# Rounded three-product projections in the first layer, with token halves kept in the gates' buffer

## The chip, the cores and the metric

The kernel runs on one core of a Trainium2 chip. The metric is the device time of one execution in microseconds. An execution's time is its span, from the first instruction to the last, and a little around it. On TensorE (PE in the profile) the matmuls run, VectorE is DVE, ScalarE is ACT, GpSimd is POOL, and SyncE is SP; SP and POOL also issue transfers (DMA).

## The reference, cut to what matters

A transformer of three layers, 512 tokens wide 1024, float32. The first layer begins so (the rest of the model is not touched):

```python
h = _rmsnorm(x, attn_norm[i])                 # 512 x 1024
proj = jnp.matmul(h, w_in[i])                 # 1024 x (512+128+512+64+8+1536+1024+1024)
q_a, c_kv, q_idx, k_idx, w_idx, qkv_b, gate_a, gate_b = _split_cols(proj)
c_kv = _rmsnorm(c_kv, kv_norm[i])
...
score = einsum("bqhs,bqh->bqs", relu(q_idx . k_idx), w_idx)
_, idx = lax.top_k(score, n_sel)              # 128 of the keys for each query
...                                           # attention on the chosen keys, a second branch with q_b, k_b, v_b
```

## The kernel before

Everything is kept transposed: a token tile is `HA[:, k]`, 128 features by 512 tokens, `k` from 0 to 7 (`DT`). The weights lie in HBM in chunks of 128 partitions by 1024 numbers (512 KB). A chunk is eight 128 x 128 blocks, the whole depth of one 128-wide output tile. SP streams the chunks into a ring of eight slots (`RING`, L333): the load of chunk n waits until the first matmul of chunk n-7 has been counted in `chunk_begun`. Chunks 0 to 5 are the compressed keys, the index keys and four index queries; 6 to 9 the queries of branch a; 10 to 21 queries, keys and values of branch b; 22 holds the two small matrices `uk` and `uv`.

What TensorE does, in its program's order (`body` of the tensor block):
- `norm_sum` (L474), then six calls of `linear` (L463): a bank of PSUM gets eight float32 matmuls of 128x128 weights by 512 tokens. The first tile waits for each normed tile (`fresh`).
- 32 small matmuls with `WIDX` (L493), a norm (L498), the bias vector (L502), the index scores (L514, 24 matmul groups, each waiting for ScalarE and VectorE), and eight flips of the bias rows (L521), which read `BIAS_FLIPPED`.
- 12 calls of `linear` (queries of both branches, keys of branch b), then four value chunks (L530). For values the tokens are the stationary side and the weights move: 32 matmuls a chunk that move 128 columns each.
- The `ukuv` chunk (L542 to L551), then the first attention (L1038 to L1067).

A float32 matmul shows as two records in the trace. ScalarE moves each finished bank out (`evac`, L1236); `bank()` lets TensorE start on a bank when its last content has been moved out (four banks in turn).

VectorE norms the tokens (`rms`, L1662), scales the small product, folds the index scores (L1722, L1724), and then takes the 128 highest per query in a long chain of its own (L1734 `max`, L1735 `match_replace`, three score tiles). It needs the first layer's projections again only at L1874. GpSimd loads constants, sends the bias vector to HBM and back (L2212, L2215), masks the scores (L2200) and then waits for `staged` (L2222), set by VectorE at L1874.

Later parts of the kernel (the second and third layer's feed-forward, L743 and L756, and the retention layer, L946 and L991) already compute in three rounded products. There a weight chunk is split into a high half, rounded to the type fp32r by ScalarE (`high`, L1609), and a low half, the difference, made by GpSimd in the chunk's own ring slot (`low`, L2324). TensorE then adds high x high, low x high and high x low (`take_parts` waits for `w_lo`). The halves of the tokens are made once, by ScalarE (high) and VectorE (low, L1704). The high halves of weights have two or four slots; `high` waits, by `chunk_begun` or by the place where it stands, until a slot's last user is done.

Areas: all big tiles share one buffer of 34688 numbers per partition (`area`, and `part` for the fp32r view of the same memory). `GATES` is at 11264 to 19455, written only in the first attention (L1894); `QB` and `KB` at 5120 to 9215, `KA` and `VA` at 19456 to 23551, `WIDX` at 19456.

```python
            def high(n, i=None, place=IN_MLP, slots=None):          # L1603, ScalarE
                turn, back = n // SLOTS + 1, (slots or len(place[0])) - 2
                act.wait_ge(chunk_full[n % SLOTS], (turn if i is None else i + turn) * 16)
                if slots is None or slots > 0:
                    act.wait_ge(S["chunk_begun"], n - back if i is None else i * SLOTS + n - back)
                fn(high_slot(n, place), RING[:, n % SLOTS], ACT.Copy).then_inc(S["w_hi"], 1)

            def low(n, place):                                      # L2321, GpSimd
                pool.wait_ge(S["w_hi"], w.next("w_hi"))
                g.tensor_tensor(RING_LOW[:, n % SLOTS], RING[:, n % SLOTS], high_slot(n, place), ALU.subtract).then_inc(S["w_lo"], 1)
```

## Time and profile before

| what | us |
|---|---|
| median of 3 runs (2671.18 to 2673.55) | 2673.55 |
| the profiled execution, its own time | 2677.25 |
| its span | 2675.5 |
| TensorE busy | 2537.1 (95% of the span) |
| VectorE busy | 814.1 (30%) |
| ScalarE busy | 693.5 (26%) |
| GpSimd busy | 596.5 (22%) |
| mean granted TensorE clock | 0.964 of full |

Starts and durations in the rows are in microseconds from the start of the span. The duration of a matmul's record is its latency; as matmuls overlap, the rate is read from a run of them (length of the run by count) or from the distance of two events that follow one tile each. "<-X" after an idle time names what ended the wait.

### The profile page before, as it was taken

What the parts mean: (1) busy time and instruction counts of PE and PEld (TensorE: products, weight loads), DVE (VectorE), ACT (ScalarE), POOL (GpSimd) and SP (SyncE); (2) the same over time, 40 slices, a digit from 0 to 9 for tenths busy, and PEclk for the clock granted to TensorE, in tenths of its full rate; (3) what the DMA queues carried; (4) which work ended last, traced back from release to release, by engine and by line L of the source; (5) the groups of instructions that cost most, each with busy time, mean ns of one, the idle gap of its engine ahead of it and who ended that gap; (6) DMA issues with size and microseconds to landing.
All of it is one profiled execution on the core that took longest, in us unless ns stands there. A gap on an engine that the chain in (4) does not pass through costs nothing.

```text
span 2675.5 us, 29863 instructions
## 1 busy us (share of the span) xinstructions
PE 2537.1 (95%) x11592; PEld 1722.2 (64%) x11592; DVE 814.1 (30%) x1327; ACT 693.5 (26%) x1116; POOL 596.5 (22%) x362
## 2 busy tenths in 40 slices
PE   7999999999799979998999999999999999999998
PEld 3446444445333334785689999989877567777876
DVE  0552431112211122235137216135100232740622
ACT  1302333401111121145332112132322232421222
POOL 0000001110111100011014444334443015344441
PEclk9699999998899989999999999999999999999999
DMA  4121000033689952220012222222222012222221
GB/s 142 48 79 59 32 32 24 32 140 152 232 357 361 382 233 71 75 78 10 16 56 95 87 87 94 79 79 103 92 84 77 24 40 87 79 87 94 94 87 39
DMA packets 68264, 275.38 MB, mean 103 GB/s; under 512 B 12440, under 2 KB 12568, under 8 KB 55872
## 3 DMA queue, kind: packets, MB, share of 16 engines
q1 hardware_dynamic: 59648, 260.01, 26.9%
q0 software_dynamic: 8512, 13.89, 1.5%
q8 instruction: 77, 1.26, 0.2%
q14 instruction: 27, 0.22, 0.0%
HBM read 321.02 MB, written 16.80 MB: 126 GB/s over the span
## 4 chain that ended last, share of the span: by engine, by line
PE 89%; issue 4%; DVE 3%; ACT 2%; POOL 2%; DMA 1%; DVEq 0%; SPq 0%; POOLq 0%; ACTq 0%
PE ps L756 15%; PE ps L743 14%; PE ps L463 7%; PE ps L1164 6%; PE ps L729 6%; PE ps L946 4%; PE ps L991 3%; PE ps L1186 3%; PE ps L1124 3%; PE ps L642 2%; PE ps L973 2%; PE ps L1049 2%; PE ps L474 2%; POOL weights_low L2324 2%; PE ps L1106 1%
## 5 line engine op out<-in xcount | busy, mean ns | idle before, releaser
L2324 POOL TENSOR_TENSOR weights_low<-weights,parts 128x1024 fp32r<-128x1024 f32 x192 | 481.8, 2512 | 907.3 <-ACT parts L1609 907.3
L756 PE MATMUL ps<-parts 128*128 128x512 f32 x1344 | 424.5, 396 | 9.0 <-DVE parts L1858 6.7
L743 PE MATMUL ps<-parts 128*128 128x264 f32 x2240 | 410.0, 285 | 8.1 <-DVE parts L1858 6.9
L743 PEld LDWEIGHTS ps<-parts 128*128 128x128 f32 x2240 | 348.4, 189 | 8.7 <-issue 8.7
L743 PE MATMUL ps<-parts,weights_low 128*128 128x264 f32 x1120 | 318.7, 285 | 0.0
L1609 ACT ACTIVATE parts<-weights 128x1024 fp32r<-128x1024 f32 x192 | 202.0, 1056 | 432.4 <-PE ps L743 143.7
L756 PEld LDWEIGHTS ps<-parts 128*128 128x128 f32 x1344 | 254.7, 190 | 70.7 <-issue 10.4
L756 PE MATMUL ps<-parts,weights_low 128*128 128x512 f32 x672 | 267.3, 398 | 0.0
L743 PEld LDWEIGHTS ps<-parts,weights_low 128*128 128x128 f32 x1120 | 212.6, 190 | 0.0
L1164 PE MATMUL ps<-area,normed 128*64 128x512 f32 x752 | 172.2, 599 | 1.6 <-DVE normed L2055 1.6
L1858 DVE TENSOR_TENSOR parts<-normed,parts 128x528 f32 (+1 forms) x64 | 155.0, 2421 | 9.6 <-DVE normed L1857 1.8
L756 PEld LDWEIGHTS ps<-parts,weights_low 128*128 128x128 f32 x672 | 127.2, 189 | 29.5
L1164 PEld LDWEIGHTS ps<-area,normed 128*64 128x64 f32 x752 | 55.9, 138 | 112.3 <-issue 110.1
L463 PE MATMUL ps<-normed,weights 128*128 128x512 f32 x288 | 124.1, 593 | 3.1 <-DVE normed L1662 2.4
L1670 DVE SCALAR_TENSOR_TENSOR residual<-residual,ps 128x528 f32<-128x528 f32 (+1 forms) x32 | 22.3, 696 | 284.7 <-PE ps L743 90.1
L463 PEld LDWEIGHTS ps<-normed,weights 128*128 128x128 f32 x288 | 54.6, 190 | 72.6 <-issue 70.1
L946 PE MATMUL ps<-parts 128*128 128x512 f32 (+1 forms) x320 | 99.8, 393 | 0.8 <-ACT area L1427 0.8
L729 PE MATMUL ps<-residual,weights 128*128 128x264 f32 x416 | 95.1, 391 | 2.6 <-DVE residual L1662 2.4
L1236 ACT ACTIVATE area<-ps 128x512 f32<-128x512 f32 (+2 forms) x71 | 42.2, 598 | 194.2 <-PE ps L463 115.7
L729 PEld LDWEIGHTS ps<-residual,weights 128*128 128x128 f32 x416 | 80.0, 193 | 18.4 <-issue 4.5
L1186 PE MATMUL ps<-area 128*64 128x512 f32 x376 | 87.7, 598 | 1.3 <-DVE area L2063 1.3
L1668 DVE TENSOR_TENSOR residual<-residual,ps 128x512 f32<-128x512 f32 (+1 forms) x32 | 21.5, 690 | 211.2 <-PE ps L743 85.1
(391 smaller groups left out, 3241.3 us busy)
## 6 DMA issues: line engine op xcount, KB each, us to landing
weights<-in_weights SPq DMA_DIRECT2D x283, 512.0 KB, 3.4
area<-in_experts SPq DMA_DIRECT2D x141, 1024.0 KB
area<-pair_rows SPq DMA_DIRECT2D x4, 1024.0 KB, 8.0
residual<-in_x SPq DMA_DIRECT2D x1, 2048.0 KB, 9.3
area<-bias_scratch POOLq DMA_DIRECT2D x1, 2048.0 KB, 8.5
token_rows<-area SPq DMA_DIRECT2D x1, 2048.0 KB, 7.0
out_tiles<-residual SPq DMA_DIRECT2D x4, 512.0 KB, 2.8
area<-in_decay POOLq DMA_DIRECT2D x2, 528.0 KB, 3.8
```

The lines of the kernel that those rows point to most:

```text
L463: ins = mm(ps[:, b], wt[:, k], rhs(k), start=k == 0, stop=k == DT - 1)
L729: ins = mm(ps[:, b + h, 0:HALF], wt[:, k], rhs(m * DT + k)[:, HALF * h:HALF * h + HALF], start=m == k == 0, stop=m == len(chunks) - 1 and ...
L743: ins = mm(ps[:, b + h, 0:HALF], wt[:, k], x[:, m * DT + k, HALF * h:HALF * h + HALF], start=m == k == j == 0, stop=m == chunks - 1 and k ...
L756: ins = mm(ps[:, b], wt[:, k], x[:, m * DT + k, META:T2], start=m == k == j == 0, stop=m == chunks - 1 and k == DT - 1 and j == 2)
L946: ins = mm(ps[0:kw, banks[j]], x[:, 2 * m + k, c:c + kw], wt[:, 512 * k:512 * k + 512], start=m == k == n == 0, stop=m == 3 and k == 1 and ...
L991: ins = mm(ps[:, 1 + n % 6], wt[:, k], y, start=m == k == j == 0, stop=m == 1 and k == DT - 1 and j == 2)
L1124: ins = mm(ps[:, 7], gate.wt[:, k], HA[:, k], start=k == 0, stop=k == DT - 1)
L1164: ins = mm(ps[WIN * side:WIN * side + WIN, n % 2], XW[n % 2][:, 4 * j + k, WIN * side:WIN * side + WIN], wt, start=j == k == 0, stop=j == ...
L1186: ins = mm(ps[WIN * side:WIN * side + WIN, 4 + h], HIDT[n % 2][:, f, WIN * side:WIN * side + WIN], wt, start=f == 0, stop=f == 1)
L1609: fn(high_slot(n, place), RING[:, n % SLOTS], ACT.Copy).then_inc(S["w_hi"], 1)
L1858: v.tensor_tensor(FL[:, at, first:T2], f, FH[:, at, first:T2], ALU.subtract).then_inc(S["dve_evac"], 1)
L2324: g.tensor_tensor(RING_LOW[:, n % SLOTS], RING[:, n % SLOTS], high_slot(n, place), ALU.subtract).then_inc(S["w_lo"], 1)
```

## The change

The first two projections stay in float32. The other sixteen tiles, and the values, are computed in three rounded products. ScalarE rounds the eight normed token tiles into `HH`, VectorE makes the differences `HL`; both lie where the gates come later. `high` and `low` are called for chunks 2 to 21, with two slots for the high halves (`IN_FIRST`, where `KA` and `VA` come later). A value chunk is laid out anew in HBM: it holds two of the eight depth blocks for all 512 value columns, so that the weights move in 512 columns, and the four banks (one per token tile) are filled over all four chunks. `BIAS_FLIPPED` moves to 5120.

```diff
-        BIAS_FLIPPED = area(11264, HEADS, SEQ)
+        BIAS_FLIPPED = area(5120, HEADS, SEQ)
...
+        HH, HL = part(11264, DT, SEQ), part(15360, DT, SEQ)
+        IN_FIRST = [[part(20480 + D * j, D) for j in range(2)], None]
...
+            def linear_split(high, low, place):
+
+                b = bank()
+                wh, wl = take_parts(place)
+                for k in range(DT):
+                    for j, (wt, x) in enumerate(((wh, high), (wl, high), (wh, low))):
+                        ins = mm(ps[:, b], wt[:, k], x[:, k], start=k == j == 0, stop=k == DT - 1 and j == 2)
+                        if k == j == 0:
+                            begun(ins)
+                ins.then_inc(S["tile_done"], 1)
...
-                for n in range(6):
+                for n in range(2):
                     linear(hn, take(), fresh=n == 0)
+                pe.wait_ge(S["x_hi"], w.next("x_hi", DT))
+                pe.wait_ge(S["x_lo"], w.next("x_lo", DT))
+                for n in range(4):
+                    linear_split(HH, HL, IN_FIRST)
...
                 for _ in range(12):
-                    linear(hn, take())
-                for _ in range(4):
-                    wt, b = take(), bank()
+                    linear_split(HH, HL, IN_FIRST)
+                banks = [bank() for _ in range(QT)]
+                for m in range(4):
+                    wh, wl = (x.rearrange("p k c -> p (k c)") for x in take_parts(IN_FIRST))
                     for t in range(QT):
-                        for k in range(DT):
-                            ins = mm(ps[:, b, P * t:P * t + P], HA[:, k, P * t:P * t + P], wt[:, k],
-                                     start=k == 0, stop=k == DT - 1)
-                            if t == k == 0:
-                                begun(ins)
-                    ins.then_inc(S["tile_done"], 1)
+                        for k in range(2):
+                            for n, (x, wt) in enumerate(((HH, wh), (HL, wh), (HH, wl))):
+                                ins = mm(ps[:, banks[t]], x[:, 2 * m + k, P * t:P * t + P], wt[:, 512 * k:512 * k + 512],
+                                         start=m == k == n == 0, stop=m == 3 and k == 1 and n == 2)
+                                if t == k == n == 0:
+                                    begun(ins)
+                        if m == 3:
+                            ins.then_inc(S["tile_done"], 1)
...
                 inverse_deviation(SEQ, D, "eps1")
+                for t in range(DT):
+                    act.wait_ge(S["norm_out"], w.next("norm_out"))
+                    fn(HH[:, t], HA[:, t], ACT.Copy).then_inc(S["x_hi"], 1)
+                for n in (2, 3):
+                    high(n, place=IN_FIRST, slots=-1)
                 for n, out in enumerate([CKV, KI] + [QI[:, j] for j in range(4)]):
                     evac(out, bank(n))
+                    if n >= 2:
+                        high(n + 2, place=IN_FIRST, slots=-1)
...
-                n = 0
-                for j in range(4):
-                    evac(QA[:, j], bank(n + j), scale=QK_SCALE)
-                for j in range(4):
-                    evac(QB[:, j], bank(n + 4 + j), scale=QK_SCALE)
-                for j in range(4):
-                    evac(KB[:, j], bank(n + 8 + j))
-                for j in range(4):
-                    evac(VB[:, :, P * j:P * j + P], bank(n + 12 + j).rearrange("p (t c) -> p t c", t=QT))
+                for n, out in enumerate([x[:, j] for x in (QA, QB, KB) for j in range(4)]):
+                    evac(out, bank(n), scale=QK_SCALE if n < 8 else 1.0)
+                    high(n + 8, place=IN_FIRST, slots=-1)
+                for n in (20, 21):
+                    high(n, place=IN_FIRST)
+                for t in range(QT):
+                    evac(VB[:, t], bank(t))
...
                 rms(8, SEQ, "attn_norm", lambda t: XA[:, t], lambda t: HA[:, t])
+                for t in range(DT):
+                    dve.wait_ge(S["x_hi"], w.next("x_hi"))
+                    v.tensor_tensor(HL[:, t], HA[:, t], HH[:, t], ALU.subtract).then_inc(S["x_lo"], 1)
...
                 pool.dma_start(WIDX, a["w_idx"]).then_inc(S["small_in"], 16)
+                for n in range(2, 8):
+                    low(n, IN_FIRST)
                 pool.wait_ge(S["bias_dram"], w.next("bias_dram"))
...
                     keep(SCORES[t][:, P * t:P * t + P], CAUSAL, LOW).then_inc(S["score_cut"], 1)
+                for n in range(8, 22):
+                    low(n, IN_FIRST)
...
-    chunks = [blocks(x) for x in (ckv, np.concatenate([kidx, kidx], 1), qidx, qa, qkv)]
+    chunks = [blocks(x) for x in (ckv, np.concatenate([kidx, kidx], 1), qidx, qa, qkv[:, :1024])]
+    chunks.append(qkv[:, 1024:].reshape(4, 2, P, 512).transpose(0, 2, 1, 3))
```

## Rows read from the trace of the kernel before

**Rows 1.** The page: TensorE's busy time, and the chain that ended last by engine.
```profile
PE 2537.1 (95%) x11592; PEld 1722.2 (64%) x11592; DVE 814.1 (30%) x1327; ACT 693.5 (26%) x1116; POOL 596.5 (22%) x362
...
PE 89%; issue 4%; DVE 3%; ACT 2%; POOL 2%; DMA 1%; DVEq 0%; SPq 0%; POOLq 0%; ACTq 0%
```

**Rows 2.** The chain in order of time, 0 to 330 us (start, length, what).
```profile
26.32 41.44 PE ps L463 x96
...
119.23 82.67 PE ps L463 x192
201.89 28.60 PE ps L530 x256
230.52 0.61 ACT area L1236
231.17 3.70 PE ps L542 x8
```

**Rows 3.** Timeline of ScalarE, 26 to 56 us: one eviction per float32 tile.
```profile
33.46 0.60 ACT L1236 ACTIVATE area<-ps 128x512 f32<-128x512 f32 x1 [8.16 <-PE ps L463]
40.33 0.60 ACT L1236 ACTIVATE area<-ps 128x512 f32<-128x512 f32 x1 [6.27 <-PE ps L463]
```

**Rows 4.** Timeline of ScalarE, 1899 to 1936 us: tiles of 24 rounded products, two slots.
```profile
1903.40 0.60 ACT L1427 ACTIVATE area<-ps 128x512 f32 x1 [4.19 <-PE ps L756]
1903.90 1.05 ACT L1609 ACTIVATE parts<-weights 128x1024 fp32r<-128x1024 f32 x1
1908.96 0.60 ACT L1427 ACTIVATE area<-ps 128x512 f32 x1 [4.01 <-PE ps L756]
```

**Rows 5.** Timeline of GpSimd, 1899 to 1936 us: the low half for the same tiles.
```profile
1905.03 2.40 POOL L2324 TENSOR_TENSOR weights_low<-weights,parts 128x1024 fp32r<-128x1024 f32 x1 [3.33 <-ACT parts L1609]
```

**Rows 6.** The chain in order of time, 1790 to 2260 us: runs of rounded products.
```profile
1936.70 39.20 PE ps L756 x168
...
1976.68 110.71 PE ps L946 x480
...
2186.94 73.07 PE ps L991 x321
```

**Rows 7.** Timeline of VectorE, 24 to 34 us: the eight norm operations.
```profile
25.42 5.39 DVE L1662 SCALAR_TENSOR_TENSOR normed<-residual,vectors,rstd 128x512 f32<-128x512 f32 x8 [25.42 <-ACT rstd L1232]
```

**Rows 8.** Timelines of GpSimd and VectorE, 1408 to 1416 us: both on two-input operations.
```profile
1408.19 5.55 POOL L2324 TENSOR_TENSOR weights_low<-weights,parts 128x1024 fp32r<-128x1024 f32 x2 [49.48 <-ACT parts L1609]
...
1408.81 2.68 DVE L1858 TENSOR_TENSOR parts<-normed,parts 128x528 f32 x1
1411.41 2.90 DVE L1856 TENSOR_TENSOR parts<-normed 128x528 f32 x1
```

**Rows 9.** One stretch: PE, PEld, DVE, ACT, POOL busy, granted clock, DMA share, GB/s.
```profile
20.00:25.00 5.00, 3.92 (x10) 1.41 (x8) 0.00 (x0) 1.01 (x2) 0.00 (x0) 1.00 0.18 72
```

**Rows 10.** Timeline of VectorE around its long chain: begin, end, next work.
```profile
109.72 0.43 DVE L1734 MAX8 small<-area 128x8 f32<-128x256 f32 x1
...
170.46 0.43 DVE L1736 TENSOR_SCALAR area<-area 128x512 f32<-128x512 f32 x1
239.24 0.76 DVE L1874 COPY area<-area 128x512 f32 x2 [68.36 <-ACT area L1236]
```

**Rows 11.** Timelines of GpSimd and VectorE, 109 and 1333 to 1346 us.
```profile
109.83 0.29 POOL L2200 TENSOR_SCALAR_AFFINE_SELECT area<-area 128x128 f32<-128x128 f32 x1 [11.01 <-DVE area L1724]
...
1342.92 2.35 POOL L2324 TENSOR_TENSOR weights_low<-weights,parts 128x1024 fp32r<-128x1024 f32 x1 [5.57 <-ACT parts L1609]
...
1344.11 0.71 DVE L1670 SCALAR_TENSOR_TENSOR residual<-residual,ps 128x528 f32<-128x528 f32 x1 [5.74 <-PE ps L729]
1344.85 0.99 DVE L1677 TENSOR_TENSOR rstd<-rstd,residual 128x528 f32<-128x528 f32 x1
```

**Rows 12.** Stretches of 66 to 122 us, columns as in rows 9.
```profile
72.00:74.00 2.00, 2.00 (x16) 2.00 (x15) 0.00 (x0) 0.00 (x0) 0.00 (x0) 0.73 0.00 0
...
112.00:114.00 2.00, 2.00 (x4) 0.76 (x3) 1.86 (x7) 0.60 (x1) 0.00 (x0) 0.53 0.00 0
```

More of the change, by code:

```diff
@@ L1351, in body @@
                 ALL, EVEN, ODD = slice(0, P), slice(0, HD), slice(HD, P)
-                act.wait_ge(S["norm_out"], w.next("norm_out", 8 + 1 + 24))
+                act.wait_ge(S["norm_out"], w.next("norm_out", 1 + 24))
                 for out in (PQ[:, 0], PQ[:, 1], PKV):
```

## The prediction

> **What bounds the kernel now.** I read the page first: TensorE is busy 95% of the span and makes up 89% of the chain that ended last [rows 1]. So a microsecond taken from TensorE's own work counts in full if nothing else is late in its place. Then the chain in order of time over the first 330 us: it runs through the very instructions that the change replaces. From 26.32 us TensorE works through six projection tiles without a gap, from 119.23 through twelve more, from 201.89 through the four value chunks, and only then an eviction of 0.61 stands in the chain [rows 2]. Then I looked for places in the same trace where the new form already runs, and for the covers: the two engines that make the halves, the loads, and the work of VectorE that goes on beside.
>
> **The change part by part.**
>
> *Sixteen tiles.* A float32 tile costs what lies between two evictions that follow one tile each: 40.33 - 33.46 = 6.87 us [rows 3]. A tile of 24 rounded matmuls over 512 tokens costs 1908.96 - 1903.40 = 5.56 us [rows 4], or 0.232 us a matmul. Other runs of the same shape give 39.20/168 = 0.233 and 73.07/321 = 0.228 [rows 6], so a tile is 5.46 to 5.60. Gain 6.87 - 5.56 = 1.31 a tile: 5.2 us for the four early ones, 15.7 for the twelve.
>
> *Values.* Now 28.60 us for 128 matmuls of 128 columns [rows 2]. Afterwards 4 chunks x 4 token tiles x 2 depths x 3 products = 96 matmuls that move 512 columns. The retention layer's values have this form, 110.71/480 = 0.2306 us each [rows 6]: 22.1 us. Gain 6.5.
>
> *A rule beside that.* What the rows show is 0.231 for a rounded matmul, but 6.87/32 = 0.215 for each of the four passes that a float32 matmul is made of. The Trainium skill (TensorE: Matmul & The Clock Gate, section Back-to-back issue gap) gives N/2.4 + 2.5 ns, 216 ns at 512 columns. By it the rounded tile would be an estimated 5.2 us and the sum some 7 us better. The passes agree with it, the rounded products of this trace do not. I take the rows of the same form; the other is a rival below.
>
> *Making the weight halves.* Per chunk ScalarE adds 1.05 us after the eviction, and GpSimd 2.4 us. In the retention stage the same two slots and nearly the same order show the whole path. The eviction begins at 1903.40, the high half at 1903.90 [rows 4], the low half at 1905.03, and it ends at 1907.43 [rows 5]. That is 4.0 us after the eviction began. The two-slot scheme lets chunk n+2 start only after tile n; meanwhile TensorE has tile n+1, 5.56 us. So the halves are ready about 1.3 us early: cost nothing. If GpSimd needed more than 1.3 us more per chunk, every us beyond that would be shared by two tiles. The queue order there holds too. On GpSimd lows 2 to 7 stand ahead of the bias transfer. Low 7 comes after tile 5 and takes until about 4 us later, while the bias vector in the trace is ready some 13 us after it; nothing waits. Lows 8 to 21 stand ahead of `staged`, which comes after all of them. On ScalarE high 7 stands ahead of the square of the compressed keys, 1 us later, behind which TensorE has 8.6 us of small matmuls. Cost nothing.
>
> *Loads.* All eight first chunks must have landed by 31 us, when high 2 begins. The transfers are done within 20 to 25 us (share 0.18, 72 GB/s) [rows 9]. Refills are asked for six tiles ahead, 33 us even at the new pace, for 512 KB. Nothing. The chunks number the same, and no transfer is added.
>
> *The token halves, the one wait that is added ahead of tile 2.* VectorE's norm ends at 30.8 [rows 7]. ScalarE's eight roundings follow each norm tile and end at about 31.5, then highs 2 and 3 until about 33.6. VectorE makes eight differences, 0.67 us each by the pace of the norm row, which has the same size: 5.4 us, to 36.3. But they read two tiles from SBUF, as the low half on GpSimd does, and such pairs collide. With two low halves on GpSimd, two operations of VectorE took 2.68 and 2.90 in place of 0.7, one per low half [rows 8]. Lows 2 and 3 fall just into these differences, so up to 2 x 2.3 us are added: the last difference is done at about 40.9. TensorE ends tile 1 at 26.32 + 2 x 6.87 = 40.1. So it stalls about 0.8 us. Bounds: 0 (no collision) to 2 us (GpSimd's halves also wait in turn).
>
> *The banks of the values.* `bank()` is called four times ahead of the first value matmul, so tile 17 must have been evicted. At the end of the values now, TensorE waits from 230.52 to 231.17 for such an eviction [rows 2]. Against back-to-back work it is 0.39 of latency + 0.65 - 0.23: 0.8 us lost. Bounds 0.6 to 1. The four evictions at the end stay four, the last as late as now. High 20 and 21 wait for `chunk_begun` in place of an eviction, 0.6 us less: covered.
>
> *Flips and clock.* The bias rows at another address cost nothing: QB and KB are written later. TensorE's granted clock falls around 73 us, in the small matmuls, and comes back around 113 [rows 12]. Both lie between the two groups of tiles and move with them. Where exactly the change of level falls against the work may differ: I allow 1 us either way.
>
> *VectorE's long chain.* It runs from 109.72 to 170.9, and its next work is at 239.24, 68 us later [rows 10]. It starts 4.3 us earlier now. Sixty us of it lie beside low halves. Were all of its operations blocked during each 2.4 us in 5.56, it would end near 206, and L1874 comes at about 213: still covered, with little left.
>
> **Sum.** 5.2 + 15.7 + 6.5 - 0.8 - 0.8 = 25.8 us. Against the profiled execution, 2677.25, that is 2651.5. Its own time lies 3.7 above the median of the runs; against the median, 2673.55, it is 2647.8, and 25.8 is 1.0%. Behind the values everything (attention, the experts) begins after this chain and moves with it. Between the ends of all bounds: with tiles of 5.46, no collision and clock luck 29.5 us, with 5.60, 2 us of stall and clock against it 22.5 us.
>
> **Rivals.**
> - *The rate of the passes.* Rounded products with this code run at 0.215. Tiles 5.15, values 20.6: 16 x 1.72 + 8.0 - 1.6 = 33.9 us, 2640. Against: three stages of rounded products in this trace, none below 0.228 [rows 6]. Chance 0.04.
> - *Late low halves.* VectorE's chain keeps GpSimd waiting for each low half, and the 1.3 us of slack is used up. Its operations are up to 0.7 us long, so at most one of them is waited for at a time; that fits into the slack. If two got in ahead each time, a chunk would be late by 0.1 to 1 us over the eight tiles beside the chain: up to 4 us in all, about 2651 to 2652. What speaks against: in rows 8 GpSimd's second low half came in right after one operation of VectorE. Chance 0.13.
> - *GpSimd shut out, the slow side.* The chain's operations follow each other with almost no gap. If they held off GpSimd as long as they go on, low 8 would wait for the chain's end. The chain ends at 166.6 in the new time, while TensorE would need chunk 8 at 126: 40 us of idle TensorE. 2647.8 + 40 = 2688. It decides from 26 us of waiting on. Against it are two observations [rows 11]: a mask on GpSimd ran inside a `max` of 0.43 without lengthening either, and an operation of VectorE with one side in PSUM kept its 0.71 beside a low half of 2.35, while the one with two SBUF tiles right behind it took 0.99. The Trainium skill (SBUF — State Buffer, section Who interferes with whom) says that a VectorE instruction with at most one SBUF input does not contend with GpSimd, and one with two does, as an exclusive lock; the trace agrees as far as these rows go. For `max` beside a long low half no row exists. Chance 0.03.
> - *Given back.* The moved work meets something fixed in time later on (an expert load, a wait that I didn't see), and half is lost: 2660. The chain behind the values is TensorE's own, so I see no candidate. Chance 0.04. That the change doesn't do what it says (the products running at float32's pace) would be slower by far; rows 6 exclude it for both forms.
>
> **The numbers.** The forecast has 0.76: 2647.8, by itself 2644 to 2651. With the late halves above and run spread (2.4 us between the runs before) the range is 2643 to 2653; it leaves out the passes' rate, the part given back and the slow side, and a little at the edges. A measurement of this kernel tells about 0.2%, 5.3 us. Faster by more than that: forecast, rate, late halves and nearly all of the fourth, 0.95; within it 0.02; slower 0.03.
>
> **What the changed profile would show.** Evictions in both projection stages 5.56 apart from the third tile on. TensorE idle about 1 us at 40 us, released by VectorE's eighth difference. Two of these differences at 2.7 to 2.9. The last of the twelve tiles ending near 181.5, the values taking 22.1 and ending near 204.6 (before 230.5). One gap under 1 us ahead of the values. VectorE's `max` and `match_replace` as long as now. The prediction is wrong if TensorE waits for `weights_low` inside the second stage, if the evictions stand further than 5.6 apart, or if the first attention doesn't begin some 26 us earlier.

## The result, and the profile after

The first column is the first measurement, on which the account below rests; the other two are repeats of both kernels, each beside the experiments of its time.

| | first measurement | repeat 1 | repeat 2 |
|---|---|---|---|
| before, median us | 2672.64 (2671.18 to 2673.55, 4 runs) | 2673.12 (2671.12 to 2675.39, 9) | 2673.25 (2668.85 to 2688.49, 11) |
| after, median us | 2646.38 (2642.52 to 2648.76, 4 runs) | 2645.91 (2642.31 to 2646.98, 4) | 2647.87 (2644.62 to 2649.32, 5) |
| ratio, 95% interval | 0.9889 [0.9859, 0.992] | 0.99 [0.9884, 0.9915] | 0.9899 [0.9877, 0.9922] |

The kernel is about 1% faster: 25 to 27 us between the medians, whose quotients are 0.9902, 0.9898 and 0.9905. The ratios of the table are not these quotients, they come with their intervals from the measurement; all three intervals lie below 1. The profiled execution after took 2648.76 us. Its page first (the span, then TensorE and the other engines, then the chain by engine):

```profile
span 2646.7 us, 29854 instructions
...
PE 2507.0 (95%) x11560; PEld 1733.2 (65%) x11560; DVE 820.3 (31%) x1335; ACT 718.1 (27%) x1144; POOL 647.7 (24%) x382
...
PE 67%; issue 4%; DVE 2%; POOL 2%; ACT 1%; DMA 1%; SPq 0%; DVEq 0%; POOLq 0%; ACTq 0%
```

Against [rows 1] TensorE's busy time fell by 30.1 us and the span by 28.8: the saving is work of TensorE, and nearly all of it arrives in this pair of executions. (The chain's share of PE is smaller than before only because the view could not follow the chain through the first part of this execution.) The evictions of ScalarE are the ruler for the changed stages, as in [rows 3]. Five evictions of the early stage (two float32 tiles, then three of the four rounded ones), then the last two of the twelve tiles, then the first and the last of the values:

```profile
36.01 0.60 ACT L1256 ACTIVATE area<-ps 128x512 f32<-128x512 f32 x1 [1.67 <-PE ps L465]
42.88 0.60 ACT L1256 ACTIVATE area<-ps 128x512 f32<-128x512 f32 x1 [6.27 <-PE ps L465]
48.36 0.60 ACT L1256 ACTIVATE area<-ps 128x512 f32<-128x512 f32 x1 [4.88 <-PE ps L476]
53.80 0.60 ACT L1256 ACTIVATE area<-ps 128x512 f32<-128x512 f32 x1 [3.89 <-PE ps L476]
...
64.68 0.60 ACT L1256 ACTIVATE area<-ps 128x512 f32<-128x512 f32 x1 [3.89 <-PE ps L476]
...
177.93 0.60 ACT L1256 ACTIVATE area<-ps 128x512 f32<-128x512 f32 x1 [3.89 <-PE ps L476]
183.37 0.60 ACT L1256 ACTIVATE area<-ps 128x512 f32<-128x512 f32 x1 [3.89 <-PE ps L476]
...
202.19 0.60 ACT L1256 ACTIVATE area<-ps 128x512 f32<-128x512 f32 x1 [5.45 <-PE ps L549]
...
206.27 0.60 ACT L1256 ACTIVATE area<-ps 128x512 f32<-128x512 f32 x1 [0.76 <-PE ps L549]
```

Of the kernel before, the sixth tile's eviction and that of the last of the twelve:

```profile
67.79 0.60 ACT L1236 ACTIVATE area<-ps 128x512 f32<-128x512 f32 x1 [6.27 <-PE ps L463]
...
201.93 0.60 ACT L1236 ACTIVATE area<-ps 128x512 f32<-128x512 f32 x1 [6.27 <-PE ps L463]
```

The float32 tile is 42.88 - 36.01 = 6.87, as before. A rounded tile is 5.44 (53.80 - 48.36), without a break in both stages. From the second eviction to the sixth (42.88 to 64.68) it is 21.80, before 67.79 - 40.33 = 27.46: **5.7 us**. The twelve tiles gain 12 x 1.43 = **17.1**. From the last of the twelve to the last eviction of the values it is 206.27 - 183.37 = 22.90 against 28.59 before (201.93 to 230.52): **5.7**. Together 28.5 us.

Yet the values' end itself, 230.52 in [rows 2], has moved by only 24.25 us in this execution. The difference lies in the first float32 tiles and the small matmuls, which nobody edited. The stretches (columns as in [rows 9]) show it, first the kernel changed, then one stretch of the kernel before:

```profile
26.00:28.00 2.00, 0.70 (x1) 0.50 (x2) 1.60 (x3) 1.06 (x3) 0.00 (x0) 0.76 0.00 0
28.00:30.00 2.00, 2.00 (x4) 0.68 (x3) 2.00 (x4) 1.90 (x4) 0.00 (x0) 0.50 0.00 0
30.00:32.00 2.00, 2.00 (x6) 0.95 (x5) 2.00 (x4) 1.90 (x4) 0.00 (x0) 0.88 0.00 0
68.00:70.00 2.00, 2.00 (x12) 2.00 (x11) 0.00 (x0) 0.17 (x1) 0.65 (x1) 0.50 0.00 0
```
```profile
28.00:30.00 2.00, 2.00 (x6) 0.93 (x5) 2.00 (x4) 0.00 (x0) 0.00 (x0) 1.00 0.00 0
```

The granted clock stood at 0.50 (the lower level, 1.2 GHz) from 28 to 30 us, as the first tile began; in the kernel before, all four stretches were at 1.00 (2.4 GHz). That first tile cost 1.6 us more. The fall that [rows 12] show at 72 us had come by 68, and the 32 small matmuls (64 records, L510, before L493) took 10.3 us instead of 8.6. The norm of VectorE started 1.0 later. 1.6 + 1.7 + 1.0 = 4.3, which is what 28.5 - 24.25 leaves. The low clock on the first tile stands in nine of the thirteen profiles of kernels with the change, and not in the one profile of the kernel before; whether the change brings it on, these profiles can't tell. In the first repeat the first tile ran at full clock, and the chain in order of time could be followed (start, length, what):

```profile
26.75 13.97 PE ps L465 x32
40.72 21.80 PE ps L476 x96
62.52 9.39 PE ps L510 x64
...
114.05 65.59 PE ps L476 x288
180.51 22.02 PE ps L549 x96
203.20 3.70 PE ps L562 x8
```

These answer to [rows 2]: 65.59/288 = 0.2277 us for a rounded matmul with 512 token columns, 22.02 us for the values, and between 179.64 and 180.51 the gap of 0.87 that was foreseen. The values' end is 28 us earlier there.

From the last eviction of the values to the end of the span it is 2445.0 us in the profile before and 2440.4, 2437.7 and 2443.2 in the three profiles of the kernel changed. That work was not edited. The one profiled execution of the kernel before was itself 4.0 to 4.6 us above the medians of the table, so these 2 to 7 us are not put down to the change.

### The profile page after: what moved, and what is told of

It is laid out like the page before. It is cut to its first block, busy times and chain, and to the rows that moved or that the text cites. A ratio compares the mean times of both kernels' runs of the same rounds, so it can differ in the third digit from the quotient of the medians.

```text
span 2646.7 us, 29854 instructions
## 1 busy us (share of the span) xinstructions
PE 2507.0 (95%) x11560; PEld 1733.2 (65%) x11560; DVE 820.3 (31%) x1335; ACT 718.1 (27%) x1144; POOL 647.7 (24%) x382
## 4 chain that ended last, share of the span: by engine, by line
PE 67%; issue 4%; DVE 2%; POOL 2%; ACT 1%; DMA 1%; SPq 0%; DVEq 0%; POOLq 0%; ACTq 0%
PE ps L776 15%; PE ps L763 14%; PE ps L1184 6%; PE ps L749 6%; PE ps L966 4%; PE ps L1011 3%; PE ps L1206 3%; PE ps L662 2%; PE ps L993 2%; POOL weights_low L2356 2%; PE ps L487 1%; PE ps L913 1%; PE ps L929 1%; PE ps L982 1%; PE ps L791 1%
## 5 line engine op out<-in xcount | busy, mean ns | idle before, releaser
L2356 POOL TENSOR_TENSOR weights_low<-weights,parts 128x1024 fp32r<-128x1024 f32 x212 | 532.9, 2516 | 1005.1 <-ACT parts L1634 1005.1
L776 PE MATMUL ps<-parts 128*128 128x512 f32 x1344 | 423.7, 395 | 9.0 <-DVE parts L1886 6.8
L1634 ACT ACTIVATE parts<-weights 128x1024 fp32r<-128x1024 f32 x212 | 222.9, 1056 | 442.2 <-PE ps L763 145.0
L2228 POOL TENSOR_SCALAR_AFFINE_SELECT area<-area 128x128 f32<-128x128 f32 x68 | 19.9, 293 | 281.8 <-DVE area L1964 201.6
L1884 DVE TENSOR_TENSOR parts<-normed 128x528 f32 (+1 forms) x64 | 49.2, 768 | 103.5 <-ACT normed L1649 55.6
L476 PE MATMUL ps<-parts 128*128 128x512 f32 x256 | 79.7, 391 | 0.7 <-ACT area L1295 0.7
```

What stands on the lines that cost most here:

```text
L476: ins = mm(ps[:, b], wt[:, k], x[:, k], start=k == j == 0, stop=k == DT - 1 and j == 2)
L776: ins = mm(ps[:, b], wt[:, k], x[:, m * DT + k, META:T2], start=m == k == j == 0, stop=m == chunks - 1 and k == DT - 1 and j == 2)
```

## Experiments

Seven of the runs below were executed four to six times, each beside the kernel before on the same chip; of the other five there is one execution each, so that their whole times say little and their rows have to carry the reading. The first run was repeat 1 above.

> The changed kernel once more, unedited, timed in five rounds. My account of the profiles: the edited stages give 28.4 us by their own rows (tiles 5.44 apart, values 22.9 from the last tile's eviction to their own last), and the rest of the difference is where TensorE's clock happens to fall and rise. Then the ratio should be 0.989 to 0.990 (27 to 30 us), and in a second profile the tiles stand 5.44 apart again, while the 1.6 us that the first float32 tile took longer in the first profile (half clock from 27 to 30 us) come and go. Rival, the forecast's sizes as they stood: 25.8 us, ratio 0.9903, tiles 5.56. Second rival, an effect of the change on later stages: the same later stretches are shorter or longer by the same amounts in both profiles of the changed kernel.

### Where the token columns lie

```diff
-        HH, HL = part(11264, DT, SEQ), part(15360, DT, SEQ)
+        HH, HL = (part(o, DT, T2)[:, :, B1] for o in (11264, 15488))
...
-        WIDX = area(19456, DT, 8)
+        WIDX = area(19712, DT, 8)
```

> The token halves at a stride of 528 numbers with 16 left out in front, as in the retention layer's input, whose tiles I took the 5.56 us from; nothing else. Theory A (where the moving tokens lie sets the rate of a rounded product): evictions 5.56 apart in place of 5.44, the sixteen tiles 1.9 us longer, time +1.9. Rival B (the rate hangs on something else in those stages, loops or the eviction's kind): evictions stay 5.44 apart, time the same.

(`WIDX`, the matrix of the small matmuls, had to make room, here and in the next kernel.) Token tiles 528 numbers apart and 16 further in, as the later layers have them. Timeline of ScalarE:

```profile
46.76 0.60 ACT L1257 ACTIVATE area<-ps 128x512 f32<-128x512 f32 x1 [4.96 <-PE ps L477]
52.32 0.60 ACT L1257 ACTIVATE area<-ps 128x512 f32<-128x512 f32 x1 [4.01 <-PE ps L477]
```

5.56 apart, exactly the tile of [rows 4] that the forecast had used. So the 0.12 us a tile are the placement of the token halves. The values, for which the token halves are the stationary side, became slower too: 23.38 us from the last tile's eviction to their own last one, instead of 22.90. The whole time did not tell it: 2645.77 (2642.66 to 2653.5), ratio 0.9905 [0.9891, 0.992], although 16 x 0.12 + 0.5 = 2.4 us lie between the two; that is within the spread of the runs.

A second kernel kept the stride of 512 and moved everything 16 numbers (64 bytes) up:

```diff
-        HH, HL = part(11264, DT, SEQ), part(15360, DT, SEQ)
+        HH, HL = part(11280, DT, SEQ), part(15376, DT, SEQ)
...
-        WIDX = area(19456, DT, 8)
+        WIDX = area(19712, DT, 8)
```

> The token halves at a stride of 512 numbers again, all of them 16 numbers (64 bytes) further up. With the stride of 528 the tiles stood 5.56 apart, without 5.44. Theory A (the start address of the moving columns decides, and 64 bytes off a 2 KB line is enough): 5.56 again. Rival B (the distance between the tiles decides, which is 2 KB here): 5.44.

```profile
49.22 0.60 ACT L1256 ACTIVATE area<-ps 128x512 f32<-128x512 f32 x1 [4.91 <-PE ps L476]
54.71 0.60 ACT L1256 ACTIVATE area<-ps 128x512 f32<-128x512 f32 x1 [3.95 <-PE ps L476]
```

5.49: the start alone costs 0.05 a tile, so by difference the stride costs 0.07; no kernel has the stride of 528 with even starts. (The whole time of the one execution, 2648.27 us, can't show that.) 5.44 was seen only with start and stride both multiples of 512, counted from the start of the buffer. Why was not tested.

The stage of the values says that the side which moves is not the whole of it. There the weights move, and their place is the same in all these kernels; only the stationary token halves were shifted. ScalarE's high halves of two following chunks, 24 rounded matmuls apart, first with everything 16 numbers up, then in the kernel changed:

```profile
192.05 1.06 ACT L1634 ACTIVATE parts<-weights 128x1024 fp32r<-128x1024 f32 x1 [5.47 <-PE ps L549]
197.65 1.06 ACT L1634 ACTIVATE parts<-weights 128x1024 fp32r<-128x1024 f32 x1 [4.54 <-PE ps L549]
```
```profile
190.24 1.06 ACT L1634 ACTIVATE parts<-weights 128x1024 fp32r<-128x1024 f32 x1 [5.32 <-PE ps L549]
195.68 1.06 ACT L1634 ACTIVATE parts<-weights 128x1024 fp32r<-128x1024 f32 x1 [4.38 <-PE ps L549]
```

5.60 against 5.44, a larger step than the 0.05 of the moving side (5.58 with the stride of 528). The granted clock was 1.00 in these stages in all three kernels.

The trace of the kernel before had both rates in it. The retention layer's output product, the third run of [rows 6], takes its moving columns from a buffer whose rows lie 512 apart (`mixed_high` and `mixed_low`). ScalarE's high halves there, one for each 24 matmuls:

```profile
2220.22 1.06 ACT L1609 ACTIVATE parts<-weights 128x1024 fp32r<-128x1024 f32 x1 [4.38 <-PE ps L991]
2225.66 1.06 ACT L1609 ACTIVATE parts<-weights 128x1024 fp32r<-128x1024 f32 x1 [4.38 <-PE ps L991]
```

5.44, before anything was changed.

### Values in float32 again

The value part undone alone: four chunks with 128 moving columns, one bank each.

```diff
-                banks = [bank() for _ in range(QT)]
-                for m in range(4):
-                    wh, wl = (x.rearrange("p k c -> p (k c)") for x in take_parts(IN_FIRST))
...
+                for _ in range(4):
+                    wt, b = take(), bank()
                     for t in range(QT):
...
+                        for k in range(DT):
+                            ins = mm(ps[:, b, P * t:P * t + P], HA[:, k, P * t:P * t + P], wt[:, k],
+                                     start=k == 0, stop=k == DT - 1)
```

> Only the values are undone: four float32 chunks of 128 columns as in the kernel before, no halves for chunks 18 to 21. Sum as forecast: the values' part is worth 6.5 - 0.8 = 5.7 us, so last tile's eviction to the last of the values 28.6 again in place of 22.9, and the time +5.7 over the changed kernel. Rival: the rounded tiles alone give nearly all since the values' columns were hidden, under 2 us.

Timeline of ScalarE, last of the twelve tiles and the four values' evictions:

```profile
183.83 0.60 ACT L1253 ACTIVATE area<-ps 128x512 f32<-128x512 f32 x1 [4.84 <-PE ps L476]
190.97 0.60 ACT L1253 ACTIVATE area<-ps 128x512 f32<-128x512 f32 x1 [6.55 <-PE ps L547]
...
212.41 0.60 ACT L1253 ACTIVATE area<-ps 128x512 f32<-128x512 f32 x1 [6.55 <-PE ps L547]
```

28.58 us, as before the change, against 22.90. But the median was 2646.98 (2645.54 to 2654.22; ratio 0.99 [0.9885, 0.9916]), 1.1 above its partner's. So both kernels were run once more.

> The kernel changed, once more, as the partner of the next one on the same chip. Both theories expect 2643 to 2648 and token tiles 5.44 apart.

> The kernel with float32 values, once more. In its first profile the stage of the values was 5.7 us longer (183.83 to 212.41) than in the kernel changed, yet the medians of the two differed by 1.1 us only. Theory A (the 5.7 us count in full, and the first pair of medians hid them in the spread of the clock): the median is 4 to 8 us above its partner's. Theory B (most of the 5.7 us is given back behind the values, by something fixed in time): the stage is 5.7 us longer again, the median at most 2 us above its partner's, and the lead at the values' end has shrunk by the second layer's start when both profiles have lost equally to the clock.

2651.22 (2648.2 to 2654.18), ratio 0.9911 [0.989, 0.9932], against the partner's 2647.87: 3.35 us. All 13 runs of the kernel changed have the median 2646.4, the 10 runs with float32 values 2649.3: 2.8 us. The profiles say more. From the last eviction of the values to the end of the span it is 2440.1 and 2440.0 us with float32 values, in the midst of the 2437.7 to 2443.2 of the kernel changed, so nothing larger than that spread is given back behind the values. (Both profiles with float32 values had the first tile at the low clock. The one profile of the kernel changed that had it too has a span of 2646.7 against their 2652.5 and 2652.3; the other two have 2640.3 and 2645.8.) The medians show between a fifth and three fifths of the 5.7. So the stage's 5.7 us are shown, and how much of them the whole time keeps is not settled: theory A asked for a difference of 4 to 8 and theory B for at most 2, and it is 3.35.

### Asking for the banks later

```diff
-                banks = [bank() for _ in range(QT)]
+                banks = []
                 for m in range(4):
...
                     for t in range(QT):
+                        if m == 0:
+                            banks.append(bank())
```

> The four banks of the values are asked for one by one, each ahead of its own first matmul. Forecast's term: the wait for tile 17's eviction costs 0.8 us, and without it TensorE goes on without a gap (first bank's old content was evicted three tiles before). So values 22.1 in place of 22.9 from the eviction of the last tile to their own last one, time -0.8, which is within the spread of the runs. Rival: the last chunk's halves are ready only just in time, so the wait moves to weights_low and nothing is gained.

```profile
183.95 0.60 ACT L1258 ACTIVATE area<-ps 128x512 f32<-128x512 f32 x1 [3.89 <-PE ps L476]
201.63 0.60 ACT L1258 ACTIVATE area<-ps 128x512 f32<-128x512 f32 x1 [5.45 <-PE ps L551]
...
205.71 0.60 ACT L1258 ACTIVATE area<-ps 128x512 f32<-128x512 f32 x1 [0.76 <-PE ps L551]
```

The stage is 21.76 instead of 22.90, and the wait for an eviction ahead of the values is gone from TensorE's waits. 2643.92 (2641.18 to 2644.75), ratio 0.9888 [0.9873, 0.9903]. The stage shows 1.1 us, where 0.8 had been expected; the 2.0 us between its median and its partner's are more than the stage explains, and within the spread.

### GpSimd's low halves beside VectorE

In the kernel changed the first low half and VectorE's eight differences met, but not as forecast. The timeline of VectorE:

```profile
31.71 4.90 DVE L1737 TENSOR_TENSOR parts<-normed,parts 128x512 fp32r<-128x512 f32 x8
```

And that of GpSimd:

```profile
33.48 7.63 POOL L2356 TENSOR_TENSOR weights_low<-weights,parts 128x1024 fp32r<-128x1024 f32 x2 [30.38 <-ACT parts L1634]
```

None of the eight was lengthened (680 to 684 ns). The two low halves took 7.63 instead of 4.8 together, and the first of them, 5.33 us, ended 2.2 us after VectorE's last difference, as if it had begun its 2.4 us of work only there. The loser was GpSimd, which had time. The Trainium skill (SBUF — State Buffer, section Who interferes with whom) says of VectorE's two-port modes that whoever issues first gets the shared pair for the whole instruction, and that issue order decides who blocks. The trace agrees that the two engines block each other; but the differences that VectorE began after 33.48 still went ahead of the low half, so the order of issue, as far as the records show it, did not decide between these two-input operations. Four kernels asked why. One makes VectorE wait for each difference before the next:

```diff
                     v.tensor_tensor(HL[:, t], HA[:, t], HH[:, t], ALU.subtract).then_inc(S["x_lo"], 1)
+                    dve.wait_ge(S["x_lo"], w.next("x_lo"))
```

> VectorE waits for each of its eight token differences before it issues the next; nothing else. In the changed kernel the eight stood back to back (4.90 us) and GpSimd's first low half waited for all of them (5.33 in place of 2.4), the other way round from the forecast. Theory A (what decides is the gap: VectorE keeps the shared port through a row of operations without a wait between, and gives it up at a gap): now the low halves come in, 2.4 us each, one or two differences last 2.7 to 2.9, the last difference is done near 41 (if the first float32 tile isn't slowed by the clock), and low 2 takes 2.4 to 3.1. Rival B (GpSimd always loses until VectorE's row is through, gap or not): low 2 still takes over 5 us, the differences end within 1 us of where they ended.

The timeline of VectorE, then that of GpSimd:

```profile
32.36 9.84 DVE L1737 TENSOR_TENSOR parts<-normed,parts 128x512 fp32r<-128x512 f32 x8
```
```profile
34.14 5.33 POOL L2357 TENSOR_TENSOR weights_low<-weights,parts 128x1024 fp32r<-128x1024 f32 x2 [31.03 <-ACT parts L1634]
```

With gaps both low halves got in at once: the 5.33 us are those of the two together here, and before, of the first alone. VectorE paid (the longest difference was 2.73). So the first low half is not slow by itself; the row without gaps held it off. Its last difference ended at 42.2, yet TensorE's first rounded matmul started at 43.06, right behind tile 1: the first tile was at the low clock here too, and that had given cover. 2649.78 in one run, with the kernel before at 2678.26 beside it.

Two others put eleven additions, with two operands in SBUF each, into the second stage behind the top-k, back to back or each waiting for the last:

```diff
+                for out in [R[:, 0:SEQ]] + [area(at, 512) for at in (33536, 27648, 28160, 30208, 30720, 31232, 31744, 32256, 32768)]:
+                    v.tensor_tensor(out, HA[:, 0], HA[:, 1], ALU.add)
+                step(v.tensor_tensor(area(34048, 512), HA[:, 0], HA[:, 1], ALU.add))
                 dve.wait_ge(S["act_evac"], w.next("act_evac", 30))
```

> Eleven extra additions of two SBUF tiles (512 columns, 0.68 us each) back to back on VectorE right after its top-k chain, beside the rounded tiles; their results are not used. This is the forecast's slow rival with operations that do share the port. Theory A (a row without gaps shuts GpSimd out): one low half lasts until the row ends, 5 to 8 us in place of 2.4, TensorE waits for weights_low once, 2 to 5 us (what is left after 1.3 us of slack), and the values end as much later. Rival B (they take turns): each low half waits for one addition at most, 3.1 us, and TensorE waits for nothing.

> The same eleven additions, each waited for before the next. Theory A (the gap decides): no low half over 3.1 us, no wait of TensorE for weights_low, two or three of the additions 2.5 to 3 us long, values' end as in the changed kernel. Rival B (the number of additions decides, not the gaps): as in the kernel with the row.

Back to back, the timeline of VectorE, then that of GpSimd:

```profile
172.76 7.70 DVE L1766 TENSOR_TENSOR area<-normed 128x512 f32<-128x512 f32 x9
```
```profile
175.12 2.39 POOL L2359 TENSOR_TENSOR weights_low<-weights,parts 128x1024 fp32r<-128x1024 f32 x1 [2.82 <-ACT parts L1634]
```

Here GpSimd came into the middle of the row at 175.12 and took its 2.39, and one of the nine additions took 2.88. So a row without gaps does not by itself shut GpSimd out; my theory fell. Tiles stayed 5.44 apart, 2646.84 us. With gaps the two low halves beside the additions took 2.39 and 2.66, and one of the nine additions 2.77. That run took 2672.31, and not by the additions: the values ended 22.9 us behind the last tile as ever, but the clock was at the low level later on, where the kernel changed has it at 0.94. The same stretch of the two, first with the gaps, then the kernel changed:

```profile
1186.00:1242.00 56.00, 49.57 (x126) 28.50 (x126) 29.99 (x97) 21.52 (x34) 7.63 (x8) 0.51 0.04 10
```
```profile
1186.00:1242.00 56.00, 47.09 (x210) 26.70 (x209) 33.13 (x103) 31.13 (x52) 7.66 (x8) 0.94 0.03 10
```

(0.94 - 0.51) x 56 = 24 us, an estimate, and near the 25.5 by which its span (2670.3) exceeds that of the kernel with the additions back to back (2644.8). One episode of that kind is as large as the whole change.

The last kernel of this kind tried what the differences have and the additions lack:

```diff
...
+                for t in range(DT):
+                    v.tensor_tensor(part(outs[t], 512), HA[:, t], HH[:, t], ALU.subtract)
...
+                dve.wait_ge(S["act_evac"], 18)
+                for t in range(DT):
+                    dve.wait_ge(S["x_hi"], DT)
+                    v.tensor_tensor(area(outs[t], 512), HA[:, 0], HA[:, 1], ALU.add).then_inc(S["xq"], 1)
...
```

> Two rows of back-to-back two-operand instructions on VectorE (512 columns, 0.68 us each), added while GpSimd cuts low halves every 5.44 us, with their outputs in space that nobody reads. First, behind the top-k (about 170 us): nine differences of the same kind as those of the token halves, with the rounded type as second operand and as output, without a wait or a signal between them. Second, behind the eviction of tile 17 (about 183.5 us): eight additions of plain float32, each with a wait that is already fulfilled and a signal, as the token halves' differences have, and a ninth. In the kernel changed the first low half could not start during the token halves' row of eight (it took 5.33 us with the wait in it), and in the burst kernel it could, in a row of plain additions without waits. Theory A (the rounded type keeps GpSimd out): the low half due in the first row begins only behind it, or takes 5 us or more, and the one in the second row takes 2.4 to 2.9. Theory B (the wait and the signal keep it out): the other way round. Theory C (neither; it was the moment, for instance that GpSimd was just coming from its wait for the weights): both low halves take 2.4 to 2.9 and lie within the rows. TensorE is not touched by any of them: its two low halves in stock cover 5.4 us, so tiles stay 5.44 apart and the time within 3 us of the kernel changed.

VectorE's two rows in its timeline, then GpSimd's low halves in them:

```profile
171.58 7.11 DVE L1767 TENSOR_TENSOR parts<-normed,parts 128x512 fp32r<-128x512 f32 x8
...
184.26 7.11 DVE L1772 TENSOR_TENSOR area<-normed 128x512 f32<-128x512 f32 x8 [4.97 <-issue]
```
```profile
174.32 2.62 POOL L2365 TENSOR_TENSOR weights_low<-weights,parts 128x1024 fp32r<-128x1024 f32 x1 [3.05 <-ACT parts L1634]
...
185.20 2.61 POOL L2365 TENSOR_TENSOR weights_low<-weights,parts 128x1024 fp32r<-128x1024 f32 x1 [3.05 <-ACT parts L1634]
```

Both got in, with either kind (one VectorE operation of each row took 2.89). Neither the rounded type nor waits and signals shut GpSimd out (2647.14 us). Why the very first low half waits for the whole row, in all twelve profiles that have this row without gaps, stays open. It costs TensorE nothing.

### The same placement in the third layer

If placement is what made 5.56 into 5.44, the 64 tiles of the third layer's feed-forward must gain too. Their four token tiles were put 512 apart on even places; asking late for the banks was kept.

```diff
+        PLACES = [(XH, XL, FH, FL), [Tight(part(*x)) for x in ((0, DT, SEQ), (4096, DT, SEQ), (12800, 16, SEQ), (20992, 16, SEQ))]]
...
             def pe_mlp(linear, cols):
+                XH, XL, FH, FL = PLACES[len(cols) == 1]
...
```

(`Tight` only takes the 16 leading columns out of a column range.)

> This is late_banks with one thing more: in the feed-forward of the third layer, whose 1536 rounded products read their 512 token columns out of rows 528 numbers apart, the four token tiles (high and low halves of the normed tokens and of the hidden units) lie 512 apart, each at a multiple of 512 numbers, as the first layer's do. The last runs of those products there took 89.2 us for 384 (0.2324 each), the first layer's, with their token columns on the even places, 0.2267. Theory A (the place of the moving columns alone sets the rate of a rounded product, in any stage): runs of 384 take 87.1 us instead of 89.2, so the stage loses 1536 x 0.0057 to 0.0066 = 9 to 10 us, the time is about 2634 (ratio 0.985), and the relu evictions and squares are as far behind as before. Theory B (the first layer's rate comes from something else that this stage does not have, such as lighter traffic of the other engines or of the transfers on the memory): the runs stay at 89 us and the time at late_banks' 2644 (ratio 0.989). Rival C (the products are faster but the hidden units' squares and differences on VectorE, some 3 x 0.7 us for every 5.6 us, or the weights' low halves on GpSimd become the bound): the runs are broken by waits on VectorE's or GpSimd's tiles and the time lies between, about 2640.

ScalarE's high halves, one per tile, in the kernel with late banks and in this one:

```profile
2403.30 1.06 ACT L1636 ACTIVATE parts<-weights 128x1024 fp32r<-128x1024 f32 x1 [4.50 <-PE ps L778]
2408.86 1.06 ACT L1636 ACTIVATE parts<-weights 128x1024 fp32r<-128x1024 f32 x1 [4.50 <-PE ps L778]
```
```profile
2401.34 1.06 ACT L1646 ACTIVATE parts<-weights 128x1024 fp32r<-128x1024 f32 x1 [4.38 <-PE ps L787]
2406.78 1.06 ACT L1646 ACTIVATE parts<-weights 128x1024 fp32r<-128x1024 f32 x1 [4.38 <-PE ps L787]
```

5.56 and 5.44, the same pair of numbers in another stage, with other neighbours. 64 x 0.12 = 7.7 us; the expectation of 9 to 10 had put the step at 0.0057 to 0.0066 a product, and it is 0.12/24 = 0.005. TensorE's waits for VectorE stayed (6.7 and 6.8 us). Of its three runs of 384 products one took 87.36 us, close to the 87.1 expected, the other two 88.97 and 88.95: there the granted clock stood at 0.83 in the 10 us around their start. Measured: 2636.79 (2634.14 to 2637.9), ratio 0.9855 [0.983, 0.9881]. That is about 9 us below the kernel changed. 7.1 of them are the step from the kernel with late banks, timed on another chip; no execution of one lies within the range of the other, and the size agrees with the 7.7 as far as such medians can tell.

## Where the prediction failed, and what of it held

The forecast was 2647.8 us, and the median came out at 2646.4. The gain is 26 us between the medians of the first measurement, 27 and 25 in the repeats, and 30 by the ratio of the first measurement, whose interval is some 8 us either way. The mechanism held: TensorE's own work shrank and nothing took its place. What failed is the size of the sum: 25.8 us, where the edited stages show 28.5. Two terms were wrong, both to the same side:

- **Sixteen tiles** (1.31 us each, 20.9 together): measured 1.43, 22.8. This is the step that failed most, "Gain 6.87 - 5.56 = 1.31 a tile", under-sized by 1.9 us. It took the tile of rows 4, which has the same form but token columns that lie 528 apart. The diff showed the other placement, and the third run of [rows 6] had it: 73.07/321 = 0.228, or 5.46 a tile by its own working, and 5.44 between its events. The prediction named it as one bound and took the other row.
- **The stall for the token halves** (-0.8, bounds 0 to 2): none, the lower bound. In the first repeat the differences ended at 36.05 instead of 40.9, and tile 2 followed tile 1 by 5.49. The step that failed is "Lows 2 and 3 fall just into these differences, so up to 2 x 2.3 us are added". The collision was there, but GpSimd paid for it. Why it was GpSimd stays open.

The other terms:

- **Values** (6.5): the chain shows 28.60 in [rows 2] and 22.02 in the repeat, 6.6.
- **The banks of the values** (-0.8, bounds 0.6 to 1): the gap was 0.87, and asking later gave 1.1 back. Right.
- **Making the weight halves** (cost nothing): TensorE never waited for `weights_low` here. A low half took 2.39 to 2.41 us, as in [rows 5].
- **VectorE's long chain** (covered, max as long as now): MAX8 and MATCH_REPLACE8 of 512 columns stayed at 0.70 and 0.68 beside low halves. The chain ended at 171.3, its next work was at 215.0: 44 us of cover left.
- **Clock** (1 us either way): too narrow. In the first profile the edited stages gained 28.5 and the unedited work ahead of the values lost 4.3, in the repeats about 0.5. Behind the values two executions of the kernel changed with the same values' end (202.56 and 202.57) had spans of 2640.3 and 2645.8. This, not the mechanism, is what the range had to carry.

Sum against sum: the forecast's 25.8, plus 1.9 for the tiles and 0.8 for the stall that did not come, gives 28.5. That the median lies only 1.4 us from the forecast is in part luck: the medians show 2 us less than the stages, which the spread of the clock covers, and that hides most of the two errors. Of the signs that the prediction gave for being wrong, two did not show: no wait for `weights_low` in the second stage, and no evictions further than 5.6 apart. The third, a first attention that doesn't begin some 26 us earlier, hangs on the clock: the values' end lies 24.25 us earlier in the first profile and 28 in the repeats. Of what it foresaw in the changed profile, the stall at 40 us and the two lengthened differences are missing.

Of the **rivals**, the passes' rate of 0.215 did not come: 0.2267 at best (5.44/24). By the formula of the Trainium skill (TensorE: Matmul & The Clock Gate, section Back-to-back issue gap), 216 ns at 512 columns, a tile would be an estimated 5.2 us. The page gives this as the gap of a single matmul by itself, and about 131 ns for a stream of weight loads and matmuls at 512 columns; the prediction left that out. The float32 passes come to the 216 (0.215), the rounded products to neither in any placement tried. Late low halves and GpSimd shut out did not occur: each low half of the second stage began about 3 us after the last one's end, on its high half. Of the operations at the chain's end one showed a collision. The timeline of VectorE, then that of GpSimd:

```profile
169.07 2.27 DVE L1764 TENSOR_SCALAR area<-area 128x512 f32<-128x512 f32 x1
```
```profile
168.67 2.39 POOL L2356 TENSOR_TENSOR weights_low<-weights,parts 128x1024 fp32r<-128x1024 f32 x1 [3.03 <-ACT parts L1634]
```

It took 2.27 instead of the 0.43 of [rows 10], until just after the low half's end at 171.06. The prediction had taken one SBUF input as free of contention; the section of the Trainium skill that it cited (SBUF — State Buffer, section Who interferes with whom) excepts the two-port modes, which a `tensor_scalar` can enter, and this row agrees with the exception.

## What to carry to other kernels

Where the operands of rounded matmuls come out of a shared buffer, lay their rows on even places (512 numbers apart here, starting on a multiple of 512): the same product ran in 0.2267 us instead of 0.2317, and as the stationary side too the token halves were faster so. When forecasting, take the rate only from rows whose operands also lie alike. Ask for a bank where it is first written, not for a group of banks ahead of the group. Judge a change of 1% by the stages it edits, event to event, because the medians of whole executions carry clock episodes of several us that belong to nobody's edit.

## What was not expected of the hardware

- The rate of a rounded matmul of 128x128 by 512 depends on where its operands lie. With the token halves as the moving side 24 of them took 5.44, 5.49 and 5.56 us: start and stride even, everything 64 bytes off, and rows 528 apart with the start off too. With the token halves as the stationary side it was 5.44, 5.60 and 5.58.
- Where back-to-back two-operand work of VectorE meets GpSimd's low half, either may wait. At the token halves GpSimd's first low half took 2.9 us longer, until behind the whole row; in three later rows it came in after at most a few instructions and one of VectorE's took 2.9 instead of 0.68.
- A one-input TENSOR_SCALAR took 2.27 us instead of 0.43 beside a low half that had started just before, while MAX8 and MATCH_REPLACE8, also reading SBUF, kept their 0.70 and 0.68.
- The granted clock can be at its lower level through a stretch of 56 us in one execution (0.51, 2672.31 us in all) and near full in another (0.94).
